# Four output tiles of block 1 in a hybrid decoder kernel: two pairs by seven half-size products each

## What is computed

```python
u = rms_norm(h, g_mix)
z = u @ w_in
y_lru  = rg_lru(causal_dwconv(z_lru), ...) * gelu(z_gate)
y_pool = multiscale_pool(z_pool, ...)
h = h + concatenate([y_lru, y_pool]) @ w_out      # the change is here
v = rms_norm(h, g_ffn)
up = causal_dwconv(v @ w_up)
h = h + (gelu(gate) * val) @ w_down
q = rms_norm(h, g_ple)
h = h + sigmoid(q @ w_ple_gate + b) * (p @ w_ple_proj)
return rms_norm(h, g_final)
```

## Time and profile before

| | us |
|---|---|
| median of three runs | 2144.92 (2144.70 to 2145.14) |
| the profiled execution, own time | 2146.13 |
| its span in the trace | 2144.3 |
| PE busy, share of the span | 2118.5, 99% |
| DVE busy | 1465.8, 68% |
| ACT busy | 872.8, 41% |
| block 1's out phase on PE | about 1237 to 1324 |

### The profile page before, as it was taken

The page is one execution under the profiler, slowest core; times in us unless marked ns, Lnnn a source line. Parts: engine busy times, 40 slices in busy tenths (PEclk is TensorE's granted clock), DMA queues, the critical chain, the costliest instruction groups (busy, mean ns, idle before and its releaser), DMA issues.

```text
span 2144.3 us, 24338 instructions
## 1 busy us (share of the span) xinstructions
PE 2118.5 (99%) x9298; PEld 1745.6 (81%) x9298; DVE 1465.8 (68%) x1685; ACT 872.8 (41%) x1138; POOL 368.9 (17%) x690
## 2 busy tenths in 40 slices
PE   8999999999999999999999999999999999999997
PEld 6888888888888888888888888888888888888885
DVE  7885498685858677687787743875665657574876
ACT  5764364351525344355445632531323131323343
POOL 0101002112112212111110110122222222221210
PEclk9999999999999999999999999999999999999998
DMA  5436546565657656577534354466666666666645
GB/s 223 162 143 248 189 172 226 211 260 209 239 199 265 225 207 245 202 285 259 191 119 147 99 206 125 149 191 194 195 195 189 195 195 192 193 196 194 203 159 180
DMA packets 135859, 422.24 MB, mean 197 GB/s; under 512 B 15552, under 2 KB 15680, under 8 KB 135744
## 3 DMA queue, kind: packets, MB, share of 16 engines
q0 software_dynamic: 92640, 321.96, 43.4%
q1 hardware_dynamic: 40800, 90.33, 12.8%
q10 hardware_dynamic: 2304, 8.39, 1.0%
HBM read 247.60 MB, written 173.02 MB: 196 GB/s over the span
## 4 chain that ended last, share of the span: by engine, by line
PE 97%; DVE 1%; DMA 1%; ACT 1%; issue 0%; SPq 0%; DVEq 0%; ACTq 0%
PE slot L665 46%; PE slot L824 38%; PE slot L904 11%; PE slot L732 1%; DMA XN<-xT 1%; DVE H L2167 0%; PE slot L755 0%; PE slot L766 0%; DVE wpair L1522 0%; DMA split_panels<-wpair 0%; DVE wsum L1516 0%; ACT L983 0%; SPq L563 0%; DVE WV L2138 0%; DVE H L2141 0%
## 5 line engine op out<-in xcount | busy, mean ns | idle before, releaser
L824 PE MATMUL slot<-ops,wpair 128*128 128x512 f32 x3696 | 841.9, 389 | 0.7 <-ACT WG L1235 0.4
L824 PEld LDWEIGHTS slot<-ops,wpair 128*128 128x128 f32 x3696 | 693.1, 188 | 147.5 <-ACT WG L1235 3.0
L665 PE MATMUL slot<-Uhi,wpair 128*128 128x512 f32 x1184 | 323.0, 392 | 10.2 <-DVE wpair L1522 9.5
L625 POOL DMA_DIRECT2D split_panels<-wpair x274 | 146.1, 534 | 841.0 <-DVE wpair L1522 816.0
L650 POOL DMA_DIRECT2D wpair<-split_panels x268 | 144.4, 539 | 761.8 <-PE slot L665 337.2
L665 PEld LDWEIGHTS slot<-Uhi,wpair 128*128 128x128 f32 x1184 | 223.0, 189 | 58.6 <-issue 10.4
L665 PE MATMUL slot<-f_split,wpair 128*128 128x512 f32 x1152 | 262.1, 389 | 0.0
L665 PEld LDWEIGHTS slot<-f_split,wpair 128*128 128x128 f32 x1152 | 216.2, 188 | 44.9
L904 PE MATMUL slot<-f_quarter,wpair 128*128 128x512 f32 x1008 | 229.5, 389 | 0.0
L904 PEld LDWEIGHTS slot<-f_quarter,wpair 128*128 128x128 f32 x1008 | 189.2, 188 | 39.3
L975 ACT ACTIVATE wpair<-raw 128x512 fp32r<-128x512 f32 x186 | 113.4, 624 | 255.8 <-PE slot L665 167.6
(11 more groups left out here) (202 smaller groups left out, 2353.5 us busy)
## 6 DMA issues: line engine op xcount, KB each, us to landing
split_panels<-wpair POOLq DMA_DIRECT2D x274, 512.0 KB, 4.6
wpair<-split_panels POOLq DMA_DIRECT2D x268, 512.0 KB, 3.6
raw<-panels SPq DMA_DIRECT2D x208, 256.0 KB, 4.2
wpair<-down_sums POOLq DMA_DIRECT2D x48, 256.0 KB, 2.9
wlo_sum<-down_sums POOLq DMA_DIRECT2D x48, 256.0 KB, 3.0
down_sums<-raw POOLq DMA_DIRECT2D x36, 256.0 KB, 3.2
H<-xT SPq DMA_DIRECT2D x8, 1024.0 KB, 10.9
pp_kept<-XQ ACTq DMA_DIRECT2D x16, 512.0 KB, 4.0
```

The costliest lines, as they stand in the source:

```text
L625: pool.dma_start(split_d[n], wpair[n % RING][:].bitcast(F32)).then_inc(split_kept[n % RING], 16)
L665: mm = pe.matmul(ps[:, h * BANK:(h + 1) * BANK], stat_[:, w], mov(part, h), start=first and i == 0, stop=last and i == 2)
L824: mm = pe.matmul(ps, stat_[:, w], (lo if part else hi)[:, k, :], start=first and k == 0 and i == 0, stop=k == KP - 1 and i == 2, skip_grou ...
```

## The change

Block 1's output tiles 4 to 7 are no longer four projections of 48 matmuls. They are two pairs, (4, 5) and (6, 7), each by seven products of 12 matmuls (4 tiles of k, 3 passes, 512 tokens): `out_by_seven`. Tiles 0 to 3, and all of block 0's, stay as they are.

- *Operands.* Three products read quarters of `Yhi` and `Ylo` directly. Four read differences of quarters (a quarter is four tiles by 512 tokens, 128x2048). DVE forms them from the split halves (`o_formed`: three instructions each for P5 and P7, two each for P6 and P4), ACT rounds each (`o_hi_part`) and DVE forms the rest (`o_lo_part`). They are formed once and serve both pairs. They lie in the buffer `ops`, over `Uhi`, `Ulo` and `XQ`.
- *Weights.* Block 0's out phase forms S1 to S4 of the two groups on DVE behind tiles 3 and 5 (`weight_sums`), POOL stores them, and SP's load into a raw buffer that holds a sum waits for that store. In block 1 each pair takes three plain panels and four sums; each sum is fetched by two transfers and has its lo part formed on DVE (`o_sum_lo`).
- *Results.* A pair uses one PSUM slot: the first half for P1, then P6, P7, P4 on top of it, the second half for P5, then P3 on top, then P2 afresh. DVE adds the running content to `H` after each product (`out_add`, 128x512). PE starts P6 only when P1's add is done, P3 when P5's is, P7 when P6's is, P2 when P3's is, and P4 when P7's is.
- *Order.* DVE's and ACT's lists of block 1's out phase are written anew (`second_out_phase`, `out_phase`).

The core of the diff:

```diff
+            if not b or m < OUT_SEVEN[0]:
+                projection(b, "out", m)
+            elif m in OUT_SEVEN:
+                job(b, "outs", m)
+                for name, _ in PRODUCTS:
+                    panel((b, "outs", m, name), None)
+                for name, _ in PRODUCTS:
+                    key = (b, "outs", m, name)
+                    step(*key)
+                    close(key, STEP[key], key)
...
-                        c, i, _ = SUM_RAW[r - RAW_RING]
-                        sync.wait_ge(sums_formed, 4 * (2 * c + i) + 4)
+                        sync.wait_ge(sums_formed, 4 * SUM_RAW[r - RAW_RING] + 4)
                         sync.wait_ge(sum_kept[r % RAW_RING], 16 * SUM_OUT[r - RAW_RING])
                     elif r >= RAW_RING:
                         sync.wait_ge(panel_lo, RAW_FREE[r - RAW_RING])
+                        if r - RAW_RING in SUM_LAST:
+                            sync.wait_ge(sums_formed, 4 * SUM_LAST[r - RAW_RING] + 1)
...
+            sums_behind = {PANEL[0, "down", c, i, "21"]: down_group(c, i) for c in range(BY_SEVEN) for i in range(2)}
+            sums_behind.update({PANEL[0, "out", m + 1, 1]: out_group(m) for m in OUT_SEVEN})
...
+            def out_by_seven(b, m):
+                key = (b, "outs", m)
+                for name, _ in PRODUCTS:
+                    n = PANEL[(*key, name)]
+                    pe.wait_ge(*split(n))
+                    if name == "P1":
+                        pe.wait_ge(*free(key))
+                    else:
+                        behind = {"P6": "P1", "P3": "P5", "P7": "P6", "P2": "P3", "P4": "P7"}.get(name)
+                        if behind:
+                            pe.wait_ge(out_added, o_count(m, behind))
+                        if name in O_AT:
+                            pe.wait_ge(o_ready, O_SPLIT.index(name) + 1)
+                    first = name in ("P1", "P5", "P2")
+                    ps = psum(key)[:, BANK:BLOCK] if name in ("P5", "P3", "P2") else psum(key)[:, 0:BANK]
+                    for k in range(KP):
+                        w = slice(k * P, (k + 1) * P)
+                        for i, (stat_, part) in enumerate(passes(n)):
+                            mm = pe.matmul(ps, stat_[:, w], o_operand(name, part)[:, k, :],
+                                           start=first and k == 0 and i == 0,
+                                           stop=k == KP - 1 and i == 2, skip_group_check=not first)
+                    mm.then_inc(pe_step, 1)
...
+            def o_hi_part(name):
+                act.wait_ge(o_sum, O_FORMED.index(name) + 1)
+                nc.scalar.activation(ops[:, O_AT[name], 0, :, :], o_raw[name][:], ACT.Copy
+                                     ).then_inc(o_hi, 1)
+            def p_hi_tiles(b):
+                act.wait_ge(p_in, b * 32 + 32)
+                act.wait_ge(pe_step, STEP[b, "G", GROUPS - 1, 1])
+                for k, tile in enumerate((WG, WV)):
+                    nc.scalar.activation(p_split[:, 0, k, :], tile[:, 0:BLOCK], ACT.Copy).then_inc(p_hi, 1)
             def out_phase(b):
-                for m in range(DT):
+                for m in range(OUT_SEVEN[0] if b else DT):
                     refill(b, "out", m)
+                    if b:
+                        act.wait_ge(pe_step, STEP[b, "G", GROUPS - 1, 1])
+                        if m != 1:
+                            o_hi_part(O_FORMED[max(m - 1, 0)])
                     if m == 1:
-                        act.wait_ge(p_in, b * 32 + 32)
-                        act.wait_ge(pe_step, STEP[b, "G", GROUPS - 1, 1])
-                        for k, tile in enumerate((WG, WV)):
-                            nc.scalar.activation(p_split[:, 0, k, :], tile[:, 0:BLOCK], ACT.Copy).then_inc(p_hi, 1)
+                        p_hi_tiles(b)
                     act.wait_ge(*out_of((b, "out", m)))
                     square(b, 1, m)
+                for m in OUT_SEVEN if b else ():
+                    if m == OUT_SEVEN[0]:
+                        o_hi_part(O_FORMED[-1])
+                    act.wait_ge(out_added, o_count(m, "P2"))
+                    square(b, 1, m)
+                    act.wait_ge(*out_of((b, "outs", m)))
+                    square(b, 1, m + 1)
                 ss_hi_part(b, 1)
...
+                    out_evicted(b, m)
+                    refill(b, "out", m)
+                    if m + 1 in OUT_SEVEN:
+                        weight_sums(out_group(m + 1), ("S1", "S3", "S2", "S4"))
...
+            def o_formed(name):
+                k_half, h = {"P5": (0, 1), "P6": (1, 1), "P4": (1, 0), "P7": (1, 1)}[name]
+                less = {"P5": (0, 0), "P7": (0, 1)}.get(name)
+                dst = o_raw[name][:]
+                if less:
+                    chain.link(v.tensor_tensor(dst, f32(y_quarter(0, k_half, h)), f32(y_quarter(0, *less)), ALU.subtract))
+                    chain.link(v.tensor_tensor(dst, dst, f32(y_quarter(1, k_half, h)), ALU.add))
+                    v.tensor_tensor(dst, dst, f32(y_quarter(1, *less)), ALU.subtract).then_inc(o_sum, 1)
+                    return
+                earlier = {"P6": "P5", "P4": "P6"}[name]
+                dve.wait_ge(o_sum, O_FORMED.index(earlier) + 1)
+                chain.link(v.tensor_tensor(dst, f32(y_quarter(0, k_half, h)), o_raw[earlier][:], ALU.subtract))
+                v.tensor_tensor(dst, dst, f32(y_quarter(1, k_half, h)), ALU.add).then_inc(o_sum, 1)
+            def o_lo_part(name):
+                dve.wait_ge(o_hi, O_FORMED.index(name) + 1)
+                v.tensor_tensor(ops[:, O_AT[name], 1, :, :], o_raw[name][:], f32(ops[:, O_AT[name], 0, :, :]),
+                                ALU.subtract).then_inc(o_ready, 1)
+            def o_sum_lo(b, m, name):
+                n = PANEL[b, "outs", m, name]
+                dve.wait_ge(split_in[n % RING], IN_COUNT[n])
+                v.tensor_tensor(wlo[n % RING], wlo_sum[n % RING][:], f32(whi[n % RING]), ALU.subtract
+                                ).then_inc(sum_lo, 1)
+            def out_add(b, m, name):
+                key = (b, "outs", m)
+                row, h, column = {"P1": (0, 0, 0), "P5": (1, 1, 1), "P6": (0, 1, 0), "P3": (0, 1, 1),
+                                  "P7": (1, 1, 0), "P2": (0, 0, 1), "P4": (1, 0, 0)}[name]
+                dve.wait_ge(pe_step, STEP[(*key, name)])
+                if name == "P1":
+                    dve.wait_ge(x_again[m // 2], b * 16 + 16)
+                earlier = {"P3": "P6", "P7": "P5", "P2": "P1"}.get(name)
+                if earlier:
+                    dve.wait_ge(out_added, o_count(m, earlier))
+                dst = H[:, m + row, half_of(h)]
+                v.tensor_tensor(dst, psum(key)[:, half_of(column)], dst, ALU.add
+                                ).then_inc(slot_free[SLOT[key]] if name == "P4" else out_added, 1)
+            def second_out_phase(b):
+                o_formed("P5")
+                out_evicted(b, 0)
+                o_formed("P6")
+                out_evicted(b, 1)
+                o_lo_part("P5")
+                p_lo_tiles(b)
+                ss_add(b, 1, 1)
+                o_formed("P4")
+                out_evicted(b, 2)
+                o_lo_part("P6")
+                ss_add(b, 1, 2)
+                o_formed("P7")
+                first, second = OUT_SEVEN
+                o_sum_lo(b, first, "P5")
+                out_evicted(b, 3)
+                o_sum_lo(b, first, "P6")
+                o_lo_part("P7")
+                o_lo_part("P4")
+                ss_add(b, 1, 3)
+                out_add(b, first, "P1")
+                o_sum_lo(b, first, "P3")
+                out_add(b, first, "P5")
+                o_sum_lo(b, first, "P7")
+                out_add(b, first, "P6")
+                out_add(b, first, "P3")
+                out_add(b, first, "P7")
+                out_add(b, first, "P2")
+                o_sum_lo(b, second, "P5")
+                out_add(b, first, "P4")
+                ss_add(b, 1, first)
+                o_sum_lo(b, second, "P6")
+                out_add(b, second, "P1")
+                o_sum_lo(b, second, "P3")
+                ss_add(b, 1, first + 1)
+                out_add(b, second, "P5")
+                o_sum_lo(b, second, "P7")
+                for name in ("P6", "P3", "P7", "P2"):
+                    out_add(b, second, name)
+                out_add(b, second, "P4")
+                ss_add(b, 1, second)
+                ss_add(b, 1, second + 1)
```

More of the change, by code:

```diff
@@ L260, with out_group, down_group @@
 KEPT_AT, IN_COUNT, SUM_TURN = {}, {}, {}
+GROUP_RAWS = [[RAW_AT["out", m + row, i] for row in range(2) for i in range(2)] for m in OUT_SEVEN]
+GROUP_RAWS += [[RAW_AT["down", c, i, kind] for kind in DOWN_KINDS] for c in range(BY_SEVEN) for i in range(2)]
+NGROUPS = len(GROUP_RAWS)
+def out_group(m):
+    return OUT_SEVEN.index(m)
+def down_group(c, i):
+    return len(OUT_SEVEN) + 2 * c + i
 def kept_panels():
@@ L267, in kept_panels @@
             continue
[L268 to L271, removed]
```

(27 more changed lines are left out.)

84 lines of the change are left out of this document (60 added, 24 removed).

## The result

The changed kernel takes 2150.24 us (median of nine runs, 2148.42 to 2151.91) against 2144.65 (nine runs, 2143.71 to 2145.14): a ratio of 1.0026, 95% interval 1.0017 to 1.0034. It is slower by 5.6 us. The forecast was 2150.2, slower. The profiled execution took 2149.54 us, with a span of 2147.7.

A forecast was written before the change was run, and what follows sets the result against it. It took PE, busy 99%, to bound the kernel. Terms -5.44 + 0.6 + 7.6 + 2.5 = +5.3 us on the median 2144.9 gave 2150.2 us, range 2146.8 to 2153.

The forecast's parts named there:

- The saving, 5.44 us: Block 1's out phase on PE: 192 matmuls become 168, saving 5.44 us if DVE stays ahead of PE.
- The wait before P5, 0.6 us: Pair (4, 5) in block 1: PE waits 0.6 us for the lo part of P5's weights.
- The wait before P6, 7.6 us: Pair (4, 5) in block 1: PE waits 7.6 us for P1's add, late in DVE's list.
- shown as released by DVE: Expected trace sign: the 7 to 8 us PE wait for P1's add would name DVE as its releaser.
- faster: Rival, chance 0.02: DVE's list before P1's add runs short and the whole 5.44 us stays, 2139.5 us.
- The clock, +2.5 us: After the wait before P6, PE's clock falls to 1.2 GHz and slow matmuls cost 2.5 us, bounds 0 and about 5.
- the clock holds: Rival, chance 0.14: PE's clock does not fall in the wait before P6; then +2.8 us, 2147.7.
- Later stalls, block 0: 0: After P6 nothing is late, and block 0's weight sums have twelve us to spare; both cost 0.
- later stalls too: Rival, chance 0.14 with block 0: late weight fetches hold adds and products, two or three of 1 us each, 2152.5.
- The end of the phase: Block 1's out phase ends with one more DVE square sum, 0.7 us later, covered by PE's next projections.
- the 3.1 us wait at the end was enough: Argument against the clock holding: in the profile before, the clock fell to 1.2 GHz within PE's 3.1 us final wait.

The follow-up runs named there:

- e3: Changed kernel with P1's add moved ahead on DVE, ACT's rounding of P7 before tile 3's square, P5's weight lo part before forming P7: 2140.25 us, ratio 0.9977.
- e1: Changed kernel with DVE's list reordered, P1's add, P3's weight lo part and P5's add ahead of two lo parts and a square sum: 2140.93 us, ratio 0.9979.
- e2: Changed kernel with only ACT's list reordered, the rounding of operand P7 ahead of the square of tile 3: 2147.47 us, ratio 1.0013.
- e4: Changed kernel with 32 filler matmuls added on PE between P5 and P6 of pair (4, 5): 2147.69 us, ratio 1.0013.
- e6: The changed kernel run once more with no edit: 2150.11 us, ratio 1.0025 against the kernel before.
- e5: Changed kernel with block 1's four projections as before, keeping only block 0's weight sums, stores and load waits: 2145.14 us, ratio 1.0002.

## Why the prediction was right

- **The saving, 5.44 us.** Right. With the waits gone (e3), 11 unheld products take 29.92 us, 2.72 each, and the stretch is 5.02 us shorter.
- **The wait before P5, 0.6 us.** Measured: P5 starts 3.36 us after P1 where 2.72 is unheld, 0.64.
- **The wait before P6, 7.6 us.** Measured: 10.34 us from P5 to P6 less 2.72, 7.62 (the view's 7.3 starts at the shown end of P5's last matmul, 1285.22). Its three parts were each as read: the order of the list (e1 takes the whole wait away), the idle time of 2.4 us for the rounding of P7 (2.33 in the timeline, 2.42 between the starts of P6 in e2 and the changed kernel, each measured from P5), and the price of each piece (2.32 linked, 2.21 unlinked; 1246.16 to 1248.48 is a linked one). The sign "shown as released by DVE" failed: the view says "issue", and only DVE's timeline and e1 show P1's add. The rival "faster" asked for pieces of 2048 columns under 1.7 us; they took 2.29. The Trainium skill (VectorE: DVE Perf Modes, The perf-mode tier table) gives float32 `tensor_tensor` from SBUF only the 1x rate, 2293 ns for 2048 elements, and the trace agrees.
- **The clock, +2.5 us.** The term was 2.5; P6 lost 5.01 - 2.72 = 2.29, and e4 gave back 2.15 of it in P6 itself. The rival "the clock holds" is refuted by the granted clock of 0.53 and by e4, which differs from the changed kernel in the work given to PE during the wait. The Trainium skill (TensorE: Matmul & The Clock Gate, Part 1: The HAM clock gate) has idleness as the cause and a return only with sustained work; e2, e4 and e6 agree: with PE idle the clock is down before P6, with PE at work it is not, and behind P6's 12 matmuls (5.08 and 5.07 us in e2 and e6) the pace is 2.72 to 2.76 us a product again.
- **Later stalls, block 0: 0.** Both right within the scatter. After P6 the products are 2.72 us apart, the first of them, P3, 2.76. The rival "later stalls too" had a real start: DVE does wait for fetched sums, three times (for the second pair's weights), by 0.3 to 0.6 us, but no add came too late for PE by it. Between e5's +0.5 and 0 the runs do not decide.
- **The end of the phase.** One more square sum behind the last add: `ss_part` starts 5.56 us after the next stage's first matmul, before 4.91 (in DVE's timelines, not among the rows shown), 0.65 later as priced, and covered.
- **The total.** 0.64 + 7.62 + 2.29 - 5.44 = 5.11 against 5.15 in the trace (the 0.04 is P3's) and 5.4 to 5.6 between medians. That the median came within 0.1 us of the forecast is partly luck. The scatter of a median here is several tenths, and the step from the profiled execution to the median, 1.2 us down as before the change, went the other way: the forecast of the profiled execution was 2151.4 us, and it took 2149.54, 0.7 below its median.

One argument for the fall was weaker than it read, that "the 3.1 us wait at the end was enough". In other executions PE waits the same 3.1 us in that place, and the clock holds. PE's timeline there, in the kernel before and in e2:

```profile
2131.09 2.08 PE L745 MATMUL slot<-AG,means 128*128 128x512 f32 x2 [3.13 <-ACT AG L1465]
...
2132.42 1.12 PE L821 MATMUL slot<-AG,means 128*128 128x512 f32 x2 [3.14 <-ACT AG L1562]
```

The granted clock of e2 in that wait and behind it, where the kernel before has 0.50 behind it:

```profile
2129.30:2132.40 3.10, 0.00 (x0) 0.00 (x0) 2.87 (x6) 2.84 (x4) 0.00 (x0) 1.00 0.45 172
2132.40:2133.60 1.20, 1.12 (x2) 0.30 (x2) 1.20 (x3) 0.02 (x1) 0.00 (x0) 1.00 0.37 145
```

The three longer waits, 4.9 us (e2) and twice 7.3 us (the changed kernel and e6), all ended at the low level, 0.50. The forecast was for a wait of 7.6 us, so its term stands; the row of the 3.1 us wait alone would not have carried it.

## What to carry to other kernels

On an engine whose list is written by hand, price the list piece by piece up to the first instruction that the bound engine waits for. A share of 68% busy says nothing about a stretch of 38 us into which 14 new pieces of 2048 columns, some 32 us, have been put. If a wait comes out, ask first whether what stands ahead of the awaited piece is needed by then: here moving three calls (two lo parts and a square sum) behind the adds was worth 9 us, more than the change could bring. And count a wait of TensorE like those here (4.9 and 7.3 us) at its length plus the slow matmuls behind it.

## What the runs showed of the hardware

- The fall of the clock costs about as much after a wait of 4.9 us (P6 5.08 us) as after 7.3 (5.01 and 5.07): 2.3 to 2.4 us over 2.72 in each.
- A wait of 3.1 us may or may not bring the fall, with the same work around it. At the end of the kernel the clock fell within the wait in the profiles of before, the changed kernel, e1 and e6, and the two matmuls behind it took 2.07 to 2.08 us. In e2 and e4 it held, and they took 1.12 and 1.13; in e3 and e5 it held to the end of the wait and fell among the two (1.65 and 1.51).
- It can be bought off: 32 matmuls whose result is thrown away kept the granted clock at 1.00 through the wait and brought 2.5 us between medians.
- A DVE instruction of 2048 columns that waits for a semaphore of the one before it starts 2.32 us after it (1246.16 to 1248.48), one that doesn't 2.21 us (from the second piece to the third). Ten forming pieces in six links pay 0.7 us for it.
